# MLP first matrix: seven block products from the third pair of columns on, block differences made in the output projections

## The chip, the cores and the metric

One core of one Trainium2 chip runs the kernel. The metric is device time in microseconds (us), the median of the runs shown. The engines are TensorE (PE: matmuls; PEld is its weight load), VectorE (DVE), ScalarE (ACT), GpSimd (POOL) and the queue of SyncE (SP), which issues the DMAs. Each engine takes its own instructions in order and waits on semaphores. They are listed by a counter's name here: `m_done` counts finished matmul units of an MLP, `m_evac` evacuated plain units, `c_done` sums of block products.

## The reference, cut to what matters

Two layers over 528 positions (16 meta tokens and 512 inputs) of width 1024. Layer 0 mixes with an mLSTM, layer 1 with differential attention; after each comes an MLP with hidden width 4096.

```python
def sq_relu_mlp(y, w_up, w_down):
    u = y @ w_up
    return jnp.square(jax.nn.relu(u)) @ w_down

for i in range(DEPTH):
    y = rmsnorm(h, norm_gains[i, 0])
    y = mixer(y)                      # mLSTM or differential attention, with its output projection
    h = h + y
    h = h + sq_relu_mlp(rmsnorm(h, norm_gains[i, 1]), mlp_w_up[i], mlp_w_down[i])
```

`rmsnorm(h, g)` is `h * rsqrt(mean(h*h) + eps) * g`; the factor of a position is called `rb` below.

## The kernel before, in words

**Number format.** Every fp32 operand is split in a high part (written by ScalarE) and a low part (what VectorE finds left), and a product is three matmuls: high x high, high x low, low x high. `yh, yl` hold the normalised input of the MLP, `ah, al` its squared activations, `hi, lo` the weights of the current pair, `raw` what DMA has loaded. Positions lie along the free dimension, 528 in layer 0 (two spans of 264), the last 512 in layer 1 (one span of 512).

**Pairs.** An MLP is 32 pairs, pair i taking 256 columns of a matrix. They come in four groups of eight: four up pairs (`is_up`, i % 8 < 4), then four down pairs. A *plain* pair is two halves m = 0, 1 of 128 columns, each 8 blocks `kb` x 3 matmuls for each span, in a PSUM bank pair or bank of its own. A *crossed* pair is made as a 2 x 2 block product with seven block products (`PRODUCTS`: A11, A12, S2, S3, S1, S4, A22), each 4 x 3 matmuls over half of the positions (264 or 256). It needs sums and differences of the weight blocks (`form`: S1 to S4, in `lof`), sums and differences of the input's blocks (`th, tl`, made from `tf`), and seven sums of products afterwards (`total`: C11, U2, U3, C22, U4, C12, C21), which put the result into `tb[0]` and `tb[1]`. Product n of a group lies in bank n % 8, so it waits for the sum that read the product eight before it.

**Which are crossed.** `crossed(i)` is an up pair with i >= PLAIN. Before, PLAIN is 8: the four up pairs of group 0 are plain, the twelve of groups 1 to 3 crossed.

**The normalisation.** In group 0 the input is unscaled: `yh, yl` are h times gain, and `evacuate` multiplies by `rb` and takes the ReLU in one operation of VectorE. During group 0 the scaled input is made as well: `scaled_y` (VectorE, `yn`), `y_forms` (VectorE, `tf`), `forms_hi` and `forms_lo` (`th`, `tl`), and at pair 4 `scaled_hi` and `scaled_lo` overwrite `yh, yl` with it. From group 1 on the products need no factor, and ScalarE takes the ReLU of the finished sums in place (`positive`, line 855). Then `squares` on ScalarE writes `abuf` and `ah`, and `act_lo` on VectorE (line 1387) writes `al` and counts `a_ready`.

**The order of the work** is written out by hand: one loop over i on each engine, with the work of neighbouring pairs interleaved. VectorE in iteration i: C21 of pair i-1, `act_lo(i-1, 0)`, `form_lo(i+1, "S23")`, C11 of pair i, `form_lo(i+1, "S14")`, U2, `act_lo(i-1, 1)`, `natural_lo(i+1)`, U3, `natural_lo(i+2)`, C22, U4, forms S1 and S3 of i+2, C12, forms S2 and S4 of i+2. For a plain pair `evacuate` stands at the place of the sums and `plain_lo` at the place of the forms. ScalarE has the high parts in the same order. The first down half of a group (`i % 8 == 4`, m = 0) waits before each block `kb` for `a_ready` of that block (line 1906 is its matmul; 1942 is that of the seven products).

**Before the MLP** stands the output projection (`out_product`): eight units of 48 matmuls (layer 0) or 24 (layer 1) on TensorE; for each VectorE adds the residual to `h`, and `norm_prep` makes `yh, yl` of the block and adds its square to `acc`. After the MLP's first half unit, TensorE sums the squares (`mean_squares`) and ScalarE makes `rb`.

## Time and profile before

| | |
|---|---|
| median of 3 runs | 1241.2 us (1240.85 to 1242.64) |
| the profiled execution | 1241.73 us |
| its span, first to last instruction | 1240.0 us |
| mean granted clock of TensorE | 0.996 of full speed |
| TensorE busy | 1206.2 us |
| VectorE busy | 858.3 us |
| ScalarE busy | 659.7 us |
| read from HBM | 107.38 MB |

All rows come from the one profiled execution. In a timeline the first number is the start in us from the span's start, the second how long it took; consecutive instructions of VectorE overlap a little, so that the spacing of their starts is about 0.08 us shorter than the duration. "Idle before" names who released an instruction that had waited.

### The profile page before, as it was taken

What the parts mean: (1) busy time and instruction counts of PE and PEld (TensorE: products, weight loads), DVE (VectorE), ACT (ScalarE), POOL (GpSimd) and SP (SyncE); (2) the same over time, 40 slices, a digit from 0 to 9 for tenths busy, and PEclk for the clock granted to TensorE, in tenths of its full rate; (3) what the DMA queues carried; (4) which work ended last, traced back from release to release, by engine and by line L of the source; (5) the groups of instructions that cost most, each with busy time, mean ns of one, the idle gap of its engine ahead of it and who ended that gap; (6) DMA issues with size and microseconds to landing.
All of it is one profiled execution on the core that took longest, in us unless ns stands there. A gap on an engine that the chain in (4) does not pass through costs nothing.

```text
span 1240.0 us, 21700 instructions
## 1 busy us (share of the span) xinstructions
PE 1206.2 (97%) x8549; PEld 1127.9 (91%) x8549; DVE 858.3 (69%) x1338; ACT 659.7 (53%) x1111; POOL 66.0 (5%) x105
## 2 busy tenths in 40 slices
PE   6999999999999999999999999998999999999997
PEld 6999999999999999999989998986787998988986
DVE  5778778667668377487468888885776774855852
ACT  4676776543526246246257787775443452543542
POOL 4121120000000000001010000000000000000000
PEclk9999999999999999999999999999999999999999
DMA  6524323232323323323122122212323232342321
GB/s 158 114 74 116 85 69 110 73 96 75 103 80 98 116 83 103 103 75 130 53 85 69 52 68 66 81 40 68 102 102 102 69 128 84 96 129 75 103 69 68
DMA packets 141600, 110.63 MB, mean 89 GB/s; under 512 B 22104, under 2 KB 139920, under 8 KB 141520
## 3 DMA queue, kind: packets, MB, share of 16 engines
q1 hardware_dynamic: 140000, 104.93, 28.1%
q0 software_dynamic: 1392, 4.49, 1.5%
q8 instruction: 56, 0.92, 0.3%
q14 instruction: 24, 0.20, 0.1%
q10 hardware_dynamic: 128, 0.09, 0.0%
HBM read 107.38 MB, written 2.13 MB: 88 GB/s over the span
## 4 chain that ended last, share of the span: by engine, by line
PE 71%; issue 19%; DVE 5%; ACT 3%; POOL 1%; DMA 1%; SPq 0%; DVEq 0%; POOLq 0%; ACTq 0%
PE ps L1906 33%; PE ps L1942 19%; PE ps L1686 15%; PE ps L1736 1%; PE ps L1754 1%; DVE tf L1436 1%; ACT wh L627 1%; DVE wl L1087 1%; DMA raw<-in_mlstm_w_in_dram 1%; DVE tbuf L1397 0%; ACT ah L867 0%; DVE tl L1449 0%; DVE lo L1295 0%; PE ps L1777 0%; PE ps L1789 0%
## 5 line engine op out<-in xcount | busy, mean ns | idle before, releaser
L1906 PE MATMUL ps<-ah,hi 128*128 128x264 f32 (+1 forms) x768 | 205.6, 322 | 3.8 <-DVE al L1387 3.8
L1906 PE MATMUL ps<-al,hi 128*128 128x264 f32 (+1 forms) x768 | 205.3, 322 | 0.0
L1906 PE MATMUL ps<-ah,lo 128*128 128x264 f32 (+1 forms) x768 | 204.8, 321 | 0.0
L627 ACT ACTIVATE hi<-raw 128x1024 fp32r<-128x1024 f32 (+1 forms) x128 | 121.5, 969 | 134.0 <-PE ps L1906 134.0
L1686 PE MATMUL ps<-yh,wh 128*128 128x264 f32 (+1 forms) x704 | 161.1, 303 | 0.0
L1686 PE MATMUL ps<-yl,wh 128*128 128x264 f32 (+1 forms) x704 | 156.0, 296 | 0.0
L1686 PE MATMUL ps<-yh,wl 128*128 128x264 f32 (+1 forms) x704 | 155.7, 295 | 0.0
L1906 PEld LDWEIGHTS ps<-ah,hi 128*128 128x128 f32 x768 | 127.4, 188 | 15.7 <-DVE al L1387 4.5
L1906 PEld LDWEIGHTS ps<-al,hi 128*128 128x128 f32 x768 | 127.5, 188 | 11.1
L1906 PEld LDWEIGHTS ps<-ah,lo 128*128 128x128 f32 x768 | 127.4, 188 | 11.1
L1401 DVE TENSOR_TENSOR h<-ps,h 128x528 f32<-128x528 f32 (+1 forms) x64 | 44.6, 697 | 110.8 <-PE ps L1906 110.8
L1686 PEld LDWEIGHTS ps<-yh,wh 128*128 128x128 f32 x704 | 112.3, 190 | 2.3
L1686 PEld LDWEIGHTS ps<-yh,wl 128*128 128x128 f32 x704 | 111.6, 189 | 2.8
L1686 PEld LDWEIGHTS ps<-yl,wh 128*128 128x128 f32 x704 | 111.8, 189 | 1.6
L1295 DVE TENSOR_TENSOR lo<-raw,hi 128x1024 fp32r<-128x1024 f32 x80 | 97.7, 1223 | 19.2 <-ACT hi L627 18.2
L1942 PE MATMUL ps<-th,hi 128*128 128x264 f32 (+1 forms) x384 | 108.5, 283 | 0.0
L1942 PE MATMUL ps<-tl,hi 128*128 128x264 f32 (+1 forms) x384 | 108.3, 282 | 0.0
L1942 PE MATMUL ps<-th,lo 128*128 128x264 f32 (+1 forms) x384 | 108.2, 282 | 0.0
L1087 DVE TENSOR_TENSOR wl<-raw,wh 128x1024 fp32r<-128x1024 f32 x64 | 79.4, 1241 | 8.1 <-ACT wh L627 6.0
L1942 PE MATMUL ps<-yh,lo 128*128 128x264 f32 (+1 forms) x288 | 81.3, 282 | 0.0
L1942 PE MATMUL ps<-yh,hi 128*128 128x264 f32 (+1 forms) x288 | 81.3, 282 | 0.0
L1942 PE MATMUL ps<-yl,hi 128*128 128x264 f32 (+1 forms) x288 | 81.2, 282 | 0.0
(267 smaller groups left out, 2613.3 us busy)
## 6 DMA issues: line engine op xcount, KB each, us to landing
raw<-in_mlp_w_up_dram SPq DMA_DIRECT2D x32, 1024.0 KB, 5.5
raw<-in_mlp_w_down_dram SPq DMA_DIRECT2D x32, 1024.0 KB, 5.2
raw<-in_diff_w_in_dram SPq DMA_DIRECT2D x24, 512.0 KB, 3.8
raw<-in_mlstm_w_in_dram SPq DMA_DIRECT2D x16, 512.0 KB, 4.6
raw<-in_mlstm_w_in_dram SPq DMA_DIRECT2D x16, 256.0 KB, 5.7
raw<-in_mlstm_w_out_dram SPq DMA_DIRECT2D x3, 1024.0 KB, 5.2
raw<-in_diff_w_out_dram SPq DMA_DIRECT2D x3, 1024.0 KB, 5.2
mbc<-gate_rows POOLq DMA_DIRECT2D x8, 264.0 KB, 5.8
```

The lines of the kernel that those rows point to most:

```text
L627: return nc.scalar.activation(o, i, ACT.Copy, scale=scale)
L1087: V.tensor_tensor(wl[:, k, :, :], raw[:, k // 2, :, P * (k % 2):P * (k % 2) + P], wh[:, k, :, :].bitcast(F32), ALU.subtract).then_inc(spli ...
L1295: V.tensor_tensor(lo[1 - i % 2][:, slots(i, m), :], raw[:, i % 2, :, P * m:P * m + P], hi[1 - i % 2][:, slots(i, m), :].bitcast(F32), ALU. ...
L1401: V.tensor_tensor(tokens(h[:, k, :], spans), src, tokens(h[:, k, :], spans), ALU.add).then_inc(m_evac, 1)
L1436: V.tensor_tensor(tf[:, f, o, 0:w], x, y, ALU.subtract).then_inc(t_made, 1)
L1686: last = mm(ps[:, bank + s, 0:w_], w[:, slot, kb, :], m[:, kb, t0:t0 + w_], start=(kb == 0 and n == 0), stop=(kb == CB - 1 and n == 2))
L1736: last = mm(ps[:, b, c:c + t1 - t0], what(rows, j), p, start=(b not in seen), stop=(n in (1, len(PIECES) - 1) and i == len(passes) - 1))
L1754: last = mm(ps[0:rows, b, c:c + t1 - t0], ks[par][:, s0:s0 + rows], q[:, t0:t1], start=(m == 0), stop=(m == 1))
L1906: last = mm(ps[:, b + s, 0:cw], x[half][:, 20 * m + kb, :], y[:, kb, c0:c0 + cw], start=(kb == 0 and n == 0), stop=(kb == CB - 1 and n == 2))
L1942: last = mm(ps[:, bank, 0:w], x[1 - i % 2][:, row + kb, :], y, start=(kb == 0 and n == 0), stop=(kb == 3 and n == 2))
```

## The change

PLAIN becomes 2: in group 0 only pairs 0 and 1 are plain, pairs 2 and 3 are crossed, 14 crossed pairs for each MLP instead of 12. The input stays unscaled for the whole MLP. Its block differences are made from h and gain by `y_forms` in the output projection, block by block: ScalarE copies `h` times gain into `thf` (two copies for each of the first four blocks), VectorE makes `tf` (one fused operation for each of the first four blocks, three for each of the last four). `forms_hi` and `forms_lo` run beside pairs 0 and 1. `scaled_y`, `scaled_hi` and `scaled_lo` are gone. The factor `rb` is applied to the finished sums: `relu` on VectorE (ReLU and product in one operation) takes the place of `positive` on ScalarE. It stands, for half 1 of pair i-1, behind `form_lo(i+1, "S23")`, and for half 0 of pair i between the forms S2 and S4 of pair i+2. The up halves of pairs 0 and 1 use fewer banks: the fourth half lies where the first was, and a half waits for the evacuation two before it (`c >= 2`). The product S2 of pair 2 waits for all four `tl` and for the evacuation of pair 1's second half.

```diff
--- before.py
+++ after.py
@@ -70,7 +70,7 @@
...
-PLAIN = 8
+PLAIN = 2
 PAIRS = 8 * GROUPS
@@ -105,7 +105,7 @@
...
 FORM = {"S1": 0, "S2": 1, "S3": 2, "A22": 3}
-UP_BANKS = [(0, 2, 4, 6, 0, 2, 4, 6), (4, 5, 7, 6, 4, 5, 7, 6)]
+UP_BANKS = [(0, 2, 4, 0), (4, 5, 4, 5)]
@@ -251,9 +251,10 @@
...
         t_at = w0[0]
+        thf = place("thf", [P, 4, 4, HALF], F32, [arena], limit)
         tl = place("tl", [P, 4, 4, HALF], F32R, w0, limit)
         tf = place("tf", [P, 4, 4, HALF], F32, [t_at], limit)
-        r0, half_at = [ring_at], w0[0]
+        r0 = [ring_at]
         hi, lo, lof = [], [], []
@@ -264,9 +265,6 @@
...
         t1 = place("t1", [P, HALF], F32, w0, limit)
-        yn = [place(f"yn{q}", [P, 2, T], F32, [at + 8 * P * 4], at + 20 * P * 4)
-              for q, at in enumerate((ring_at, ring_at + 28 * P * 4, half_at, half_at + 28 * P * 4))]
         w0 = [a_at]
@@ -337,7 +335,7 @@
...
         m_hi, m_lo, s_made, m_done, c_done, m_relu, m_evac = sems("m_hi m_lo s_made m_done c_done m_relu m_evac")
-        yn_done, t_made, th_done, tl_done, y2_hi, y2_lo, t1_done = sems("yn_done t_made th_done tl_done y2_hi y2_lo t1_done")
+        yt_done, t_made, th_done, tl_done, t1_done = sems("yt_done t_made th_done tl_done t1_done")
@@ -816,6 +814,11 @@
...
                     norm_prep(n, k, spans)
+                    if k < 4:
+                        t0, w = mlp_shape(layer)
+                        for f, n0 in ((2, t0), (3, t0 + w)):
+                            last = copy(thf[:, f, k, 0:w], h[:, k, n0:n0 + w], gains[:, 8 * n + k:8 * n + k + 1])
+                        last.then_inc(yt_done, 1)
@@ -847,12 +850,6 @@
...
                     copy(t1[:, 0:w], ps[:, bank_of(i, "A11"), 0:w]).then_inc(t1_done, 1)
-                def positive(i, m):
-                    b = 8 * (4 * layer + i // 8) + 2 * (i % 8) + m
-                    act.wait_ge(c_done, 7 * ranks + summed(i, "C21" if m else "C12"))
-                    nc.scalar.activation(tb[m][:, t0:T], tb[m][:, t0:T], ACT.Relu).then_inc(m_relu, 1)
@@ -884,16 +881,10 @@
...
-                def scaled_hi(q):
-                    act.wait_ge(yn_done, 8 * layer + 8)
-                    act.wait_ge(m_done, items + DONE[3, 1])
-                    copy(yh[:, 2 * q:2 * q + 2, t0:T], yn[q][:, :, t0:T]).then_inc(y2_hi, 1)
                 def forms_hi(n):
-                    act.wait_ge(t_made, 8 * layer + 2 * n + 2)
-                    f = (0, 2, 1, 3)[n]
+                    act.wait_ge(t_made, 16 * layer + 16)
+                    f = (2, 1, 0, 3)[n]
                     copy(th[:, f, :, 0:w], tf[:, f, :, 0:w]).then_inc(th_done, 1)
@@ -905,8 +896,6 @@
...
                         snap(i)
-                    if crossed(i - 1):
-                        positive(i - 1, 1)
                     if crossed(i + 1):
@@ -920,12 +909,9 @@
...
                         finish(i, 0)
-                    if i == 3:
-                        for n in range(4):
-                            forms_hi(n)
-                    if i == 4:
-                        for q in range(4):
-                            scaled_hi(q)
+                    if i < 2:
+                        forms_hi(2 * i)
+                        forms_hi(2 * i + 1)
                     if i + 2 < PAIRS:
@@ -934,7 +920,6 @@
...
                     if crossed(i):
-                        positive(i, 0)
                         squares(i, 0)
@@ -1304,13 +1289,28 @@
...
                     norm_prep(n, k, spans)
+                    y_forms(layer, n, k)
+            def y_forms(layer, norm, k):
+                t0, w = mlp_shape(layer)
+                kb, gain, made = k % 4, gains[:, 8 * norm + k:8 * norm + k + 1], 16 * layer
+                first, second = h[:, k, t0:t0 + w], h[:, k, t0 + w:T]
+                if k < 4:
+                    dve.wait_ge(yt_done, 4 * layer + k + 1)
+                    V.scalar_tensor_tensor(tf[:, 0, kb, 0:w], second, gain, thf[:, 2, kb, 0:w],
+                                           ALU.mult, ALU.subtract).then_inc(t_made, 1)
+                else:
+                    dve.wait_ge(t_made, made + kb + 1)
+                    for f, x, other in ((1, second, tf[:, 0, kb, 0:w]), (2, second, thf[:, 3, kb, 0:w]), (3, first, tf[:, 1, kb, 0:w])):
+                        if f == 3:
+                            dve.wait_ge(t_made, made + 4 + 3 * kb + 1)
+                        V.scalar_tensor_tensor(tf[:, f, kb, 0:w], x, gain, other, ALU.mult, ALU.subtract).then_inc(t_made, 1)
...
                 items, ranks, norm = layer * N_DONE, layer * N_CROSSED, 2 * layer + 1
-                gain = lambda kb: gains[:, 8 * norm + kb:8 * norm + kb + 1]
                 def form(i, name, after):
@@ -1320,8 +1320,6 @@
...
                     if name == "S1":
-                        if i in (8, 9):
-                            dve.wait_ge(y2_lo, 4 * layer + 4)
                         dve.wait_ge(m_raw[i % 2], 16 * (PAIRS // 2 * layer + i // 2 + 1))
@@ -1380,6 +1378,11 @@
...
+                def relu(i, m):
+                    dve.wait_ge(c_done, 7 * (ranks + RANK[i] - 1) + SUMS["C21" if m else "C12"])
+                    V.scalar_tensor_tensor(tb[m][:, t0:T], tb[m][:, t0:T], 0.0, rb[:, t0:T], ALU.max, ALU.mult).then_inc(m_relu, 1)
                 def act_lo(i, m):
@@ -1413,39 +1416,11 @@
...
-                def scaled_y(b0):
-                    dve.wait_ge(unit_done, (U_OUT0, U_OUT1)[layer] + 8)
-                    dve.wait_ge(evac, (U_OUT0, U_OUT1)[layer] + 8)
-                    dve.wait_ge(rb_ready, norm + 1)
-                    for b in range(b0, b0 + 4):
-                        V.scalar_tensor_tensor(yn[b // 2][:, b % 2, t0:T], h[:, b, t0:T], gain(b), rb[:, t0:T],
-                                               ALU.mult, ALU.mult).then_inc(yn_done, 1)
-                def y_forms(n):
-                    f = (0, 2, 1, 3)[n]
-                    if n < 2:
-                        dve.wait_ge(yn_done, 8 * layer + 8)
-                    else:
-                        dve.wait_ge(t_made, 8 * layer + (2, 6)[n - 2])
-                    for q in range(2):
-                        top, low, o = yn[q], yn[2 + q], slice(2 * q, 2 * q + 2)
-                        x, y = ((top[:, :, mid:T], top[:, :, t0:mid]), (low[:, :, mid:T], top[:, :, mid:T]),
-                                (low[:, :, mid:T], tf[:, 0, o, 0:w]), (low[:, :, t0:mid], tf[:, 1, o, 0:w]))[n]
-                        V.tensor_tensor(tf[:, f, o, 0:w], x, y, ALU.subtract).then_inc(t_made, 1)
-                def scaled_lo(q):
-                    dve.wait_ge(y2_hi, 4 * layer + q + 1)
-                    V.tensor_tensor(yl[:, 2 * q:2 * q + 2, t0:T], yn[q][:, :, t0:T],
-                                    yh[:, 2 * q:2 * q + 2, t0:T].bitcast(F32), ALU.subtract).then_inc(y2_lo, 1)
                 def forms_lo(n):
-                    f = (0, 2, 1, 3)[n]
+                    f = (2, 1, 0, 3)[n]
                     dve.wait_ge(th_done, 4 * layer + n + 1)
-                    dve.wait_ge(t_made, 8 * layer + 8)
+                    dve.wait_ge(t_made, 16 * layer + 16)
                     V.tensor_tensor(tl[:, f, :, 0:w], tf[:, f, :, 0:w], th[:, f, :, 0:w].bitcast(F32), ALU.subtract).then_inc(tl_done, 1)
@@ -1460,6 +1435,8 @@
...
                         form_lo(i + 1, "S23")
+                    if crossed(i - 1):
+                        relu(i - 1, 1)
                     if crossed(i):
@@ -1479,18 +1456,9 @@
...
                         if is_up(i):
-                            if i < 2:
-                                scaled_y(4 * i)
                             act_lo(i, 0)
-                            if i == 2:
-                                for n in range(4):
-                                    y_forms(n)
-                            if i == 3:
-                                for n in range(4):
-                                    forms_lo(n)
-                        elif i == 4:
-                            for q in range(4):
-                                scaled_lo(q)
+                            forms_lo(2 * i)
+                            forms_lo(2 * i + 1)
                     after = crossed(i + 2)
@@ -1508,6 +1476,9 @@
...
                         form(i + 2, "S2", 1)
+                    if crossed(i):
+                        relu(i, 0)
+                    if after:
                         form(i + 2, "S4", 3)
@@ -1885,10 +1856,8 @@
...
                         pe.wait_ge(evac, u_out + 5 + 2 * i + m)
-                    if c >= 4:
+                    if c >= 2:
                         pe.wait_ge(m_evac, plains + c - 1)
-                    if (i, m) == (1, 1):
-                        pe.wait_ge(ln_done, norm + 1)
                     if crossed(i - 1) and m == 0:
@@ -1914,22 +1883,24 @@
...
                         pe.wait_ge(m_lo, ready + READY[i, group])
-                    if i == 8 and name == "A11":
-                        pe.wait_ge(y2_lo, 4 * layer + 4)
-                    if i == 8 and name == "S2":
+                    if i == PLAIN and name == "A11":
+                        pe.wait_ge(ln_done, norm + 1)
+                        pe.wait_ge(evac, u_out + 8)
+                    if i == PLAIN and name == "S2":
+                        pe.wait_ge(m_evac, plains + 4)
                         pe.wait_ge(tl_done, 4 * layer + 4)
-                    if n >= 8:
+                    if n >= 8 and i - i % 8 + (n - 8) // 7 >= PLAIN:
...
                             pe.wait_ge(c_done, 7 * ranks + summed(last, FREED[product_]))
-                    elif n >= 4:
+                    elif 4 <= n < 8:
...
                         pe.wait_ge(m_evac, plains + PLAINS[u // 2, u % 2])
-                    elif n == 0 and i > 8:
+                    elif n == 0:
                         pe.wait_ge(c_done, 7 * (ranks + RANK[i] - 1))
...
                     for kb in range(4):
```

## Rows read from the trace of the kernel before

**Rows 1.** The page, part 1: busy time and share of the span, each engine.

```profile
PE 1206.2 (97%) x8549; PEld 1127.9 (91%) x8549; DVE 858.3 (69%) x1338; ACT 659.7 (53%) x1111; POOL 66.0 (5%) x105
```

**Rows 2.** The chain that ended last: start us, us, what; both MLPs.

```profile
274.17 23.37 PE ps L1906 x192
...
451.26 40.77 PE ps L1942 x336
492.03 46.76 PE ps L1906 x384
...
888.11 22.32 PE ps L1906 x96
...
974.26 39.69 PE ps L1942 x336
1013.96 44.63 PE ps L1906 x192
```

**Rows 3.** Waits of TensorE: us in total, times, longest.

```profile
PE ps L1906 <- DVE al L1387: 3.8, 2, 2.2
```

**Rows 4.** Timeline of VectorE: start us, us, instruction, idle time before it.

```profile
460.50 0.42 DVE L1381 TENSOR_TENSOR tbuf<-u,ps 128x264 f32<-128x264 f32 x1
460.84 0.68 DVE L1328 TENSOR_TENSOR lof<-lof,raw 128x512 f32<-128x512 f32 x1
...
462.17 0.42 DVE L1381 TENSOR_TENSOR tbuf<-u,ps 128x264 f32<-128x264 f32 x1
462.85 0.71 DVE L1387 TENSOR_TENSOR al<-abuf,ah 128x528 fp32r<-128x528 f32 x1 [0.25 <-ACT ah L867]
463.87 1.23 DVE L1335 TENSOR_TENSOR lo<-lof,hi 128x1024 fp32r<-128x1024 f32 x1 [0.31 <-ACT hi L627]
465.01 0.42 DVE L1381 TENSOR_TENSOR tbuf<-t,ps 128x264 f32<-128x264 f32 x1
...
467.11 0.70 DVE L1387 TENSOR_TENSOR al<-abuf,ah 128x528 fp32r<-128x528 f32 x1
467.73 0.68 DVE L1342 TENSOR_TENSOR lo<-raw,hi 128x512 fp32r<-128x512 f32 x1
468.33 0.42 DVE L1381 TENSOR_TENSOR u<-u,ps 128x264 f32<-128x264 f32 x1
...
474.03 0.71 DVE L1387 TENSOR_TENSOR al<-abuf,ah 128x528 fp32r<-128x528 f32 x1 [0.26 <-ACT ah L867]
...
494.79 0.71 DVE L1387 TENSOR_TENSOR al<-abuf,ah 128x528 fp32r<-128x528 f32 x1 [1.04 <-ACT ah L867]
...
1017.12 0.69 DVE L1387 TENSOR_TENSOR al<-abuf,ah 128x512 fp32r<-128x512 f32 x1 [1.01 <-ACT ah L867]
```

**Rows 5.** Timeline of VectorE, output projection and first pairs of the MLPs.

```profile
239.68 0.43 DVE L1098 COPY acc<-abuf 128x528 f32<-128x528 f32 x1
...
275.69 0.71 DVE L1397 SCALAR_TENSOR_TENSOR tbuf<-ps,rb 128x528 f32<-128x528 f32 x1 [1.00 <-ACT rb L663]
...
282.73 0.71 DVE L1387 TENSOR_TENSOR al<-abuf,ah 128x528 fp32r<-128x528 f32 x1 [1.25 <-ACT ah L867]
...
313.30 4.76 DVE L1449 TENSOR_TENSOR tl<-tf,th 128x1056 fp32r<-128x1056 f32 x4 [0.27 <-ACT th L627]
...
889.60 0.69 DVE L1397 SCALAR_TENSOR_TENSOR tbuf<-ps,rb 128x512 f32<-128x512 f32 x1 [2.53 <-issue]
```

**Rows 6.** Groups of instructions by form: busy us, mean ns of one.

```profile
L1258 DVE SCALAR_TENSOR_TENSOR acc<-acc,of 128x528 f32<-128x528 f32 x8 | 5.6, 701 | 0.7 <-ACT acc L779 0.7
...
L855 ACT ACTIVATE tbuf<-tbuf 128x528 f32<-128x528 f32 x24 | 15.4, 640 | 46.8 <-DVE tbuf L1381 46.8
```

**Rows 7.** Windows near the start: busy of each engine, granted clock, DMA.

```profile
core 0: us, PE busy (x) PEld busy (x) DVE busy (x) ACT busy (x) POOL busy (x), PEclk, DMA share, GB/s
...
42.00:46.00 4.00, 2.17 (x19) 1.63 (x18) 3.20 (x6) 3.74 (x9) 2.06 (x4) 1.00 0.30 69
46.00:50.00 4.00, 4.00 (x24) 3.92 (x23) 2.76 (x4) 3.87 (x10) 0.21 (x1) 0.57 1.02 236
```

## The prediction

> **What bounds the kernel now.** I read the page first: TensorE is busy 97% of the 1240.0 us span [rows 1], so only what shortens its stream, or makes it wait, moves the end. Next the chain that ended last, merged in time [rows 2]: in both MLPs it is almost nothing but TensorE. Four crossed pairs (7 block products of 12 matmuls each, 336 in all) take 40.77 us in layer 0 and 39.69 us in layer 1; eight plain halves take 46.76 and 44.63 us. Then the waits [rows 3]: in 64 pairs TensorE stood still twice, 3.8 us together, both for `al`, the low parts of the activations (once in group 0 of each layer). Last VectorE's timeline, since the change gives VectorE work. VectorE is only 69% busy over the span [rows 1], but inside four crossed pairs it goes from one operation to the next with hardly a gap: from one `al` to the corresponding one of the next pair it needs 462.85 to 474.03, 11.18 us [rows 4], while TensorE needs 40.77/4 = 10.19 us for the pair. It gains its lateness back only in the plain pairs that follow. This is the place to look at.
>
> **1. Matmuls removed.** Pairs 2 and 3 of both layers become crossed. A plain pair costs 46.76/4 = 11.69 us (layer 0) and 44.63/4 = 11.16 (layer 1), a crossed one 10.19 and 9.92 [rows 2]. Gain 1.50 x 2 + 1.24 x 2 = 5.5 us, all on TensorE's path.
>
> **2. The old wait.** The two waits of TensorE for `al` in group 0 [rows 3] came from a VectorE queue that carried `scaled_y`, the old `y_forms`, `forms_lo` and `scaled_lo` between pairs 0 and 4. Those are gone or moved ahead. Behind pair 3 VectorE's queue now holds two crossed pairs only, and if TensorE has waited in pair 2 (below), VectorE is level with it there. Gain 3.8 us.
>
> **3. Block differences in the output projections.** ScalarE gets 8 copies of 264 elements, VectorE 16 fused operations of about 0.38 us each (a 264-element sum is spaced 0.34 us, from 460.50 to 460.84 [rows 4]; a pointer scalar adds a little). VectorE gets at most three more per output block, 1.1 us, under 5.8 us of matmuls for a block, so TensorE covers it. Only the last three matter: they push VectorE's two splits of pair 1 behind them, so that the first evacuation begins at about 275.8 instead of 275.69 [rows 5]. Uncovered it would be 1.1 us per layer; the 0.1 is in part 4's sum, and layer 1 has room until its factor is ready.
>
> **4. VectorE's opening queue.** Pair 2's third product, S2, needs the evacuation of pair 1's second half, its bank; before, that half had a bank of its own and nothing waited. On VectorE it now stands behind all the preparation of pairs 2 and 3. Spacings, from one start to the next: evacuation to `al` 0.70 + 1.25 (wait for ScalarE's two squares) = 1.95 [rows 5]; `al` to the first `tl` 0.71 + 0.27 = 0.98; two `tl` 2 x 4.76/4 = 2.38; a 1024-element low part 1.14; forms S1 and S3 2 x 0.60; S2 and S4 1.33 (460.84 to 462.17) [rows 4]. A block is 8.98 us. Between the two blocks lie evacuation 0.62, two 1024-element low parts 2.28, `al` 0.62, a 512-element one 0.60: 4.12. So the evacuation of pair 1's second half starts at 275.8 + 8.98 + 4.12 + 8.98 = 297.9 and S2 may start at 298.65. TensorE is there at 274.17 + 3 x 5.85 + 2 x 1.46 = 294.6 [rows 2]. **Wait: 4.0 us.** In layer 1: 889.60 [rows 5] + 22.1 less some 0.3 for the shorter rows + 0.75 = 912.1, against 888.11 + 3 x 5.58 + 2 x 1.42 = 907.7: **4.4 us**. Together 8.4. Bounds for each: 2.5 us less if VectorE need not wait for ScalarE's squares (1.25 us, twice), 0.6 more if its steps are 2.5% longer.
>
> **5. The ReLU moves from ScalarE to VectorE.** ScalarE loses 0.64 us, VectorE gets a two-source fused operation over 528 elements; the same form, L1258, takes 0.701 us [rows 6], spacing about 0.62. What is queued behind it: `relu(i,0)` stands between the forms S2 and S4 of pair i+2, and the squares on ScalarE and then `al` wait for it. From its start to `al` is 0.70 + 1.25 = 1.95 us. From `al` of one pair to the next `relu(i,0)` there are, by the spacings of [rows 4]: 1.02 + 1.14 + 0.62 (`relu(i-1,1)`) + 0.34 + 1.14 + 0.34 + 0.62 + 0.60 + 0.34 + 1.14 + 0.68 + 1.20 + 0.34 + 0.60 = 10.12 us. So a full iteration takes 12.07 us, not 11.18, against TensorE's 10.19. Following the group that starts at 451.26: the first ReLU at 461.44, its `al` at 463.4; the second pair's at 475.5; the third (no forms to make: 7.98 to C12, 0.47 for C12 to end, 1.95) at 485.9; then ReLU and `al` of its second half, the last at 488.4; splits and sums 1.02 + 3.30 to C12 of the fourth pair at 492.75; ReLU 493.2, `al` 495.2, ReLU 495.8, last `al` 497.7, done 498.45. Before, that last `al` began at 494.79 [rows 4]: 2.95 us earlier. The first down half needs it for its eighth block, at 492.03 + 7/8 x 5.85 = 497.1 [rows 2]. The old margin of 1.6 us becomes a **wait of 1.4 us**, in each of three groups. Layer 1: last `al` at 1017.12 + 2.95, done 0.75 later at 1020.8, needed at 1013.96 + 4.88 = 1018.8: 2.0 us, and a few tenths more, as its crossed pairs are 0.27 us shorter and VectorE's steps hardly are: **2.3 us**. Together 3 x 1.4 + 3 x 2.3 = 11.1 us. From both sides: with the one-source COPY of the same 528 elements as the nearest other row, 0.43 us [rows 5], eight ReLUs would be 2.2 us shorter in the chain and about 0.8 us of the 2.95 remained, inside the margin: 0. With every step 2.5% longer it is about 5 us more than my sum. I take the fused row, the same form and size. ScalarE's idle time does not help; it waits for VectorE already.
>
> The row says that ReLU costs 0.640 us on ScalarE and 0.701 on VectorE [rows 6]. The Trainium skill, "ScalarE: Activation LUTs", Rules for kernel authors, says to use VectorE, not ScalarE, for ReLU and multiplication. By that rule the move would cost nothing and part 5 would be 0; here the form is two-source fp32 and the busier engine gets it, so I go by the row.
>
> **6. The clock.** The windows show the granted clock at 1.00 through 42 to 46 us, where TensorE was busy for 2.17 of 4 us, and 0.57 in the 4 us after, a mixture of 2.4 and 1.2 GHz [rows 7]: 0.43 x 4 = 1.7 us lost. A wait of 4 us in part 4 may cause the same, twice; in the MLP before, waits of up to 2.2 us [rows 3] did not show it. Bounds 0 and 3.4; I take one fall, 1.7 us. The Trainium skill, "TensorE: Matmul & The Clock Gate", Part 1, says that an idle array falls back to half rate; by that it would be both, 1.7 us more.
>
> **The sum.** -5.5 - 3.8 + 8.4 + 11.1 + 1.7 = +11.9 us. The span would be 1251.9, the profiled execution, 1241.73, 1253.6, and the median, which is 0.5 us lower (1241.2), **1253**. SP's loads for pairs 2 to 5 start when the last split of the buffer is done and have 5 to 7 us before use, as later groups have now; I give them nothing.
>
> **Rivals.** (a) **Forecast**, both VectorE delays reach TensorE: 0.74. (b) **Faster**: VectorE's backlog is drained before TensorE meets it, so only parts 1 and 2 count, 1241.2 - 9.3 = 1232. Place: VectorE's queue between the first evacuation and S2, and in the last of four crossed pairs. It decides when 4.0 of the 22.1 us of part 4 vanish and 1.5 of the 2.95 of part 5. For it: ScalarE is relieved, and part of VectorE's spacing is waiting for it. Against it: ScalarE's squares still follow the ReLU, and the steps are measured ones. 0.06. (c) **Only one of the two**: no wait in part 5, as with the one-source price: about 1242; or none in part 4: -9.3 + 11.1, 1243. 0.10, nearly all of it within 0.2% of 1241.2. (d) **The lateness grows**: VectorE's steps 2.5% longer put `al` late for the seventh block too, and delay the second half of pair 1: 1259 or more. [...] 0.10. That the seven products do not save their matmuls I leave out: they do so in 12 pairs per layer now [rows 2].
>
> **Range and chances.** 0.2% of the time, 2.5 us, is about what this kernel's measurement can tell. (a) alone covers 1249 to 1257: below, no fall of the clock and half of part 4's 5 us; above, two falls, 1.2 more in part 4 and 0.2 for each of the six groups. With half of (d) the range is 1247 to 1259. Faster by over 0.2%: 0.06, (b). Within: 0.08, from (c). Slower: 0.86.
>
> **What would show it.** Right: the waits view has S2 of pair 2 (th products) waiting some 4 us for VectorE, twice; six waits for `al` of 1 to 2.5 us, at the start of the down pairs of groups 1 to 3; none in group 0; crossed pairs still 10.2 and 9.9 us; ReLU on VectorE at 0.70 us; the clock below 1.00 after one of the 4 us waits. Wrong: no wait of TensorE at `al`, or VectorE reaching C21 with idle time in front of it in the second pair of a group; or waits inside the crossed pairs for banks, which I give none, since the sums stay within eight products.

## The result, and the profile after

The median of 6 runs is 1261.32 us (1259.09 to 1266.43); the kernel before, run 6 times beside it, has 1241.92 (1240.85 to 1242.79). The ratio is 1.0152, with a 95% interval of 1.0135 to 1.0169: **slower by 19.4 us**. The forecast was 1253, range 1247 to 1259. The direction was right and the time lies 2.3 us above the range.

The profiled execution took 1260.07 us, with a span of 1258.4. Page, part 1, of the kernel after:

```profile
PE 1207.8 (96%) x8597; PEld 1130.7 (90%) x8597; DVE 896.5 (71%) x1430; ACT 638.9 (51%) x1083; POOL 63.7 (5%) x105
```

Against [rows 1], VectorE has 38 us more and ScalarE 21 us less. TensorE runs 48 matmuls more (12 fewer for each new crossed pair of layer 0, 36 more, but half as wide, for each of layer 1) and is busy 1.6 us longer, though its columns are fewer: some of them run at a lower clock. Now its waits. The waits view, TensorE:

```profile
PE ps L1875 <- DVE al L1390: 11.0, 10, 1.6
PE ps L1913 <- DVE tbuf L1400: 4.2, 1, 4.2
PE ps L1913 <- issue: 4.0, 1, 4.0
...
PE ps L1875 <- DVE tbuf L1400: 0.6, 1, 0.6
```

Line 1875 is the plain matmul, 1913 that of the seven products, 1390 is `act_lo`, 1400 `evacuate`. Where [rows 3] had two waits and 3.8 us, there are 19.8 us now. Timeline of TensorE, the rows with a wait inside the MLPs (those of group 2 of layer 1, at 1114.68 and 1117.19, repeat the two of group 1):

```profile
297.95 0.56 PE L1913 MATMUL ps<-th,hi 128*128 128x264 f32 x1 [3.98 <-issue]
412.17 0.51 PE L1875 MATMUL ps<-ah,hi 128*128 128x264 f32 x2 [1.57 <-DVE al L1390]
501.62 0.51 PE L1875 MATMUL ps<-ah,hi 128*128 128x264 f32 x2 [1.58 <-DVE al L1390]
589.15 0.52 PE L1875 MATMUL ps<-ah,hi 128*128 128x264 f32 x2 [0.46 <-DVE al L1390]
591.73 0.51 PE L1875 MATMUL ps<-ah,hi 128*128 128x264 f32 x2 [1.57 <-DVE al L1390]
...
907.32 0.47 PE L1875 MATMUL ps<-yh,hi 128*128 128x512 f32 x1 [0.59 <-DVE tbuf L1400]
920.15 0.36 PE L1913 MATMUL ps<-th,hi 128*128 128x256 f32 x1 [4.17 <-DVE tbuf L1400]
1027.85 0.50 PE L1875 MATMUL ps<-ah,hi 128*128 128x512 f32 x1 [0.43 <-DVE al L1390]
1030.36 0.50 PE L1875 MATMUL ps<-ah,hi 128*128 128x512 f32 x1 [1.55 <-DVE al L1390]
...
1201.50 0.50 PE L1875 MATMUL ps<-ah,hi 128*128 128x512 f32 x1 [0.33 <-DVE al L1390]
1204.02 0.76 PE L1875 MATMUL ps<-ah,hi 128*128 128x512 f32 x1 [1.55 <-DVE al L1390]
```

The two rows at `th` are S2 of pair 2. In layer 0 the view names "issue" as what ended the wait; the evacuation that S2 waits for ended just then, as the timeline of VectorE shows (it started at 297.15). The row at 907.32 is the last of the four plain up halves of layer 1, which waits for its bank. The others are the first down half behind four crossed pairs. Its block 8, which needs the last `al`, waits 1.6 us in groups 1 to 3 of both layers, and in four of these six its block 7 has waited 0.3 to 0.5 us, 2.5 to 2.6 us earlier. Timeline of VectorE, the evacuation of pair 1's second half in each layer, and in the group that starts at 453.93 the ReLUs and low parts:

```profile
297.15 0.70 DVE L1400 SCALAR_TENSOR_TENSOR tbuf<-ps,rb 128x528 f32<-128x528 f32 x1
...
464.27 0.70 DVE L1384 SCALAR_TENSOR_TENSOR tbuf<-tbuf,rb 128x528 f32<-128x528 f32 x1
...
466.22 0.71 DVE L1390 TENSOR_TENSOR al<-abuf,ah 128x528 fp32r<-128x528 f32 x1 [0.30 <-ACT ah L864]
...
476.34 0.70 DVE L1384 SCALAR_TENSOR_TENSOR tbuf<-tbuf,rb 128x528 f32<-128x528 f32 x1
...
500.86 0.71 DVE L1390 TENSOR_TENSOR al<-abuf,ah 128x528 fp32r<-128x528 f32 x1 [1.24 <-ACT ah L864]
...
919.37 0.68 DVE L1400 SCALAR_TENSOR_TENSOR tbuf<-ps,rb 128x512 f32<-128x512 f32 x1
```

Read the two ReLUs of half 0: 476.34 - 464.27 = 12.07 us, which is VectorE's time for a crossed pair; TensorE's is 10.19. Read the last `al` from the group's first matmul: 500.86 - 453.93 = 46.93 us. Before, it was 494.79 [rows 4], and the group's first matmul is at 451.10 in the timeline (451.26 in the chain of [rows 2], which enters it a little later): 43.69, 3.24 us less. And the clock, windows of the kernel after around S2 in layer 0 (columns as in [rows 7]):

```profile
292.00:296.00 4.00, 1.97 (x17) 1.75 (x15) 4.00 (x6) 1.03 (x2) 0.00 (x0) 1.00 0.13 46
296.00:300.00 4.00, 2.05 (x9) 2.08 (x10) 3.96 (x6) 3.46 (x6) 0.00 (x0) 0.52 0.02 6
300.00:304.00 4.00, 4.00 (x24) 4.00 (x23) 2.70 (x6) 1.36 (x2) 0.00 (x0) 0.63 0.04 6
304.00:308.00 4.00, 4.00 (x35) 4.00 (x34) 3.03 (x6) 0.50 (x1) 0.00 (x0) 1.00 0.76 257
```

TensorE stands still from about 294 to 297.95, and the granted clock is 0.52 and 0.63 in the eight microseconds from 296 on: mostly the lower level, 1.2 GHz, then 2.4 GHz again. The same happens behind the 4.17 us wait of layer 1 and once more in its last group, from 1204 to 1210 (0.91 and 0.75 in two windows of 5 us). Inside the MLPs of the kernel before the clock never fell. Near the start it is the other way round: there the kernel before has the fall of [rows 7], and the windows 46 to 50 and 50 to 54 us of the kernel after are at 1.00.

**Where the 18.4 us of span went**, from the first matmuls of the stages in both traces. Fewer matmuls: -5.5. The two old waits: -4.4. The waits of S2: 4.2 and 4.3. The four plain up halves of layer 1, with the new wait of 0.59 us at 907.32: 1.0. The down pairs behind crossed ones: 1.9, 1.9 and 2.5 in layer 0, three times 2.5 in layer 1, 13.8 together. Three falls of the clock: 2.2 + 1.6 + 1.5 = 5.3. The MLP of layer 0 starts 0.65 earlier. The sum is 18.1. Whether the fall near the start has a part in the 0.65 is open: of the profiled executions here, those with one such fall (the kernel before and experiments 2, 3, 4, 6) start this MLP at 266.2 to 267.3, those with none (the kernel after and experiment 8) at 266.7.

### The profile page after: what moved, and what is told of

The parts are those of the page before. It is cut to its first block and busy times, and to the rows that moved or that the text cites. A ratio compares the mean times of both kernels' runs of the same rounds, so it can differ in the third digit from the quotient of the medians.

```text
span 1258.4 us, 21898 instructions
## 1 busy us (share of the span) xinstructions
PE 1207.8 (96%) x8597; PEld 1130.7 (90%) x8597; DVE 896.5 (71%) x1430; ACT 638.9 (51%) x1083; POOL 63.7 (5%) x105
## 5 line engine op out<-in xcount | busy, mean ns | idle before, releaser
L1913 PE MATMUL ps<-th,hi 128*128 128x264 f32 (+1 forms) x448 | 128.6, 287 | 8.2 <-DVE tbuf L1400 4.2
L1913 PE MATMUL ps<-tl,hi 128*128 128x264 f32 (+1 forms) x448 | 128.1, 286 | 0.0
L1913 PE MATMUL ps<-th,lo 128*128 128x264 f32 (+1 forms) x448 | 128.0, 286 | 0.0
L863 ACT ACTIVATE abuf<-tbuf 128x528 f32<-128x528 f32 (+1 forms) x64 | 40.9, 638 | 170.8 <-DVE tbuf L1384 164.8
L1280 DVE TENSOR_TENSOR lo<-raw,hi 128x1024 fp32r<-128x1024 f32 x72 | 87.9, 1224 | 18.8 <-ACT hi L625 17.6
L1913 PE MATMUL ps<-yh,lo 128*128 128x264 f32 (+1 forms) x336 | 94.9, 282 | 0.0
L1913 PE MATMUL ps<-yh,hi 128*128 128x264 f32 (+1 forms) x336 | 94.8, 282 | 0.0
L1913 PE MATMUL ps<-yl,hi 128*128 128x264 f32 (+1 forms) x336 | 94.7, 282 | 0.0
```

The costliest lines, as they stand in the source:

```text
L863: nc.scalar.activation(ab[m][:, t0:T], tb[m][:, t0:T], ACT.Square).then_inc(sqa_done, 1)
L1280: V.tensor_tensor(lo[1 - i % 2][:, slots(i, m), :], raw[:, i % 2, :, P * m:P * m + P], hi[1 - i % 2][:, slots(i, m), :].bitcast(F32), ALU. ...
L1913: last = mm(ps[:, bank, 0:w], x[1 - i % 2][:, row + kb, :], y, start=(kb == 0 and n == 0), stop=(kb == 3 and n == 2))
```

## The experiments

Two theories. **A**: VectorE's queue sets the end in two places, in front of S2, where bank and evacuation meet, and in front of `al`, where the ReLU stands in the way; all else follows from the order of the queue. **B**: VectorE simply has too much to do in a crossed pair, in any order, or the new products of pairs 2 and 3 are dearer than counted. The kernel before had a median of 1242.74 us beside experiments 1 to 4 and of 1242.80 us beside 5 to 8.

**1. ReLU back on ScalarE**, without the factor `rb` of these sums.

```diff
@@ ScalarE @@
+                    if crossed(i - 1):
+                        positive(i - 1, 1)
...
                     if crossed(i):
+                        positive(i, 0)
                         squares(i, 0)
@@ VectorE @@
-                    if crossed(i - 1):
-                        relu(i - 1, 1)
...
-                    if crossed(i):
-                        relu(i, 0)
```

> The changed kernel with the ReLU of the crossed pairs back on ScalarE, at its old places; the factor rb of these activations is left out. Theory A (both VectorE delays are real and separate, and the clock falls after waits): TensorE's waits for al in front of the down pairs, 11.0 us in ten, go to 0; the waits for S2 of pair 2 (8.2 us) and for the evacuation in pair 1 (0.6 us) stay, with a fall of the clock of 1.7 us behind each of the two long ones. About 1241.9 - 5.5 - 3.8 + 8.8 + 3.4 = 1245 us. Rival B (the seven products of pairs 2 and 3 save less than 5.5 us, or the work moved to the output projections costs TensorE time): the waits go as in A, but the time stays above 1250. Rival C (the waits for al come from the opening, not from the ReLU): they stay, above 1257.

Measured: 1244.83 us (1243.29 to 1247.37), ratio 1.0014 [1.0005, 1.0024]. No wait for `al` is left, S2 still waits 4.0 and 4.2 us, and the clock still falls behind both. The last `al` of a group starts at 43.70 us from the group's first matmul. So the ReLU's move to these places costs 1261.3 - 1244.8 = 16.5 us, and the rest of the change costs about 2. B's second half, dearer products, is gone: where no wait and no fall comes, pairs 2 and 3 of layer 0 take 20.37 us together (first matmuls of the stages, experiment 4), twice the 10.19 of a crossed pair.

**2. Other banks for the first pairs of layer 0, and S2 in both layers without the wait for the evacuation of pair 1's second half.**

```diff
-UP_BANKS = [(0, 2, 4, 0), (4, 5, 4, 5)]
+UP_BANKS = [(0, 2, 0, 4), (4, 5, 4, 5)]
...
-                    if c >= 2:
+                    if c >= 2 and (layer, c) != (0, 3):
                         pe.wait_ge(m_evac, plains + c - 1)
...
                     if i == PLAIN and name == "S2":
-                        pe.wait_ge(m_evac, plains + 4)
+                        pe.wait_ge(m_evac, plains + 3)
                         pe.wait_ge(tl_done, 4 * layer + 4)
+                    if i == PLAIN and name == "A22":
+                        pe.wait_ge(m_evac, plains + 4)
```

> The changed kernel with another bank for the second half of pair 1, so that S2 of pair 2 waits only for the evacuation before, and A22 of pair 2 for the last one. Theory A (VectorE's queue is behind by 4 us at this point whatever TensorE waits for): the 4 us waits at S2 go, but TensorE then meets the same lateness at the first down half of group 0, as waits for al of its seventh and eighth block, together 3.1 us in layer 0 and 3.6 in layer 1; only 1.8 us are saved, and the clock falls less often: 1256 to 1260 us. Rival B (the S2 wait is a matter of one bank): the waits go and nothing comes in their place, 1261.3 - 8.2 - 3.4 = 1249.7 us.

Measured: 1257.21 us (1255.72 to 1260.54), ratio 1.0125 [1.0109, 1.014]. The waits of S2 are gone, with 8.2 us in them, and the time fell by only 4. In layer 1 no bank was changed, and none had to be: by `UP_BANKS` that half lies in bank 5 there, and S2 of pair 2 in bank 0 (product 16, modulo 8). Its wait of 4.17 us was for a condition of the code that S2 does not need. The waits view of this kernel and its new rows in the timeline of TensorE show why:

```profile
PE ps L1875 <- DVE al L1390: 16.7, 14, 1.6
```

```profile
316.62 0.51 PE L1875 MATMUL ps<-ah,hi 128*128 128x264 f32 x2 [1.07 <-DVE al L1390]
319.19 0.81 PE L1875 MATMUL ps<-ah,hi 128*128 128x264 f32 x2 [1.57 <-DVE al L1390]
...
936.67 0.51 PE L1875 MATMUL ps<-ah,hi 128*128 128x512 f32 x1 [1.48 <-DVE al L1390]
939.18 0.51 PE L1875 MATMUL ps<-ah,hi 128*128 128x512 f32 x1 [1.54 <-DVE al L1390]
```

Group 0 had no wait for `al` after the change; it has four now, 5.7 us more in total. The wait of S2 had let VectorE catch up. Taken away, its lateness goes on to the next place where TensorE meets it: the down pairs of group 0 take 51.27 us where the kernel after has 46.76, and 49.78 in layer 1 where it has 44.63. The clock falls there too (0.88 and 0.78 in the windows from 315 to 325, 0.66 from 940 to 945).

**3. The ReLU of half 1 directly behind C21**, one step earlier in the same queue, the same work.

```diff
                         total(i - 1, "C21")
+                        relu(i - 1, 1)
...
                         form_lo(i + 1, "S23")
-                    if crossed(i - 1):
-                        relu(i - 1, 1)
```

> The changed kernel with relu(i-1, 1) one place up in VectorE's order: directly behind the sum C21 of pair i-1, ahead of act_lo(i-1, 0) and form_lo(i+1, S23). The same instructions, the same durations. Theory A (the place in the queue decides: the squares of the second half run while VectorE works on the first): the waits for al, 11.0 us, go to below 1 us, the waits for S2 stay: 1244 to 1247 us. Rival B (VectorE's total of work decides, 28 ReLUs of 0.70 us for each layer): nothing changes, 1259 us or more.

Measured: 1244.41 us (1243.58 to 1247.09), ratio 1.0014 [1.0005, 1.0024]. This one line takes 16.9 us away. The fused ReLU still runs on VectorE, 707 ns each. Timeline of VectorE of this kernel, the end of a group whose first matmul is at 451.18 (C21 of a pair, its ReLU, the two `al`):

```profile
492.15 0.43 DVE L1379 TENSOR_TENSOR tbuf<-u,ps 128x264 f32<-128x264 f32 x1 [0.20 <-PE ps L1912]
492.61 0.71 DVE L1384 SCALAR_TENSOR_TENSOR tbuf<-tbuf,rb 128x528 f32<-128x528 f32 x1
493.24 0.70 DVE L1390 TENSOR_TENSOR al<-abuf,ah 128x528 fp32r<-128x528 f32 x1
494.56 0.71 DVE L1390 TENSOR_TENSOR al<-abuf,ah 128x528 fp32r<-128x528 f32 x1 [0.63 <-ACT ah L864]
```

The ReLU of half 1 now comes before `al` of half 0, so ScalarE squares half 1 while VectorE makes that `al`. In the kernel after it came behind it, and VectorE then stood 1.24 us for ScalarE. The last `al` starts 43.38 us from the group's start instead of 46.93. A full iteration is shorter as well: the ReLUs of half 0 stand at 461.53 and 472.97, 11.44 us apart instead of 12.07. B's first half has fallen: the work is the same, the place decides. At this place the move from ScalarE costs nothing that can be told (experiment 1 has 1244.83 us), though VectorE's 11.44 are still more than TensorE's 10.19: over four pairs the lateness stays inside the margin.

**4. Experiments 2 and 3 together, the other ReLU early as well**, directly behind C12, and one low part of the second down pair behind the last `al` (beside the lines of experiments 2 and 3):

```diff
                         total(i, "C12")
+                        relu(i, 0)
                     if after:
                         form(i + 2, "S2", 1)
-                    if crossed(i):
-                        relu(i, 0)
...
                     elif 1 <= i < PAIRS - 1:
+                        if crossed(i - 1) and not crossed(i):
+                            plain_lo(layer, i + 1, 0)
                         plain_lo(layer, i + 1, 1)
...
-                    elif i + 2 < PAIRS:
+                    elif i + 2 < PAIRS and not (crossed(i) and not crossed(i + 1)):
                         plain_lo(layer, i + 2, 0)
```

> The changed kernel with four reorderings and no work added or left out: the banks of e2, the ReLU places of e3, relu(i, 0) directly behind C12, and the low part of the second pair of down columns moved behind the last al. Theory A: no wait of TensorE above 0.5 us in either MLP, no fall of the clock there: 1241.9 - 5.5 - 3.8 + 0.6 = 1233 us. Rival B (the waits come back somewhere else in VectorE's order, or the clock falls anyhow): 1237 us or more, and the waits view names the place.

Measured: 1233.43 us (1231.94 to 1233.56), ratio 0.9923 [0.9909, 0.9936]. No wait for `al` and none of S2 is left, and no clock below 1.00 inside the MLPs. This beats both kernels.

**5. The kernel before, with its ReLUs on VectorE at the places of the change.** The product with `rb` comes along, on data already scaled.

```diff
@@ ScalarE @@
-                    if crossed(i - 1):
-                        positive(i - 1, 1)
...
-                        positive(i, 0)
@@ VectorE @@
                         form_lo(i + 1, "S23")
+                    if crossed(i - 1):
+                        relu(i - 1, 1)
...
                         form(i + 2, "S2", 1)
+                    if crossed(i):
+                        relu(i, 0)
```

> The kernel before, with one part of the change alone: the ReLU of the crossed pairs on VectorE with the factor rb, at the two places of the change (the activations are already scaled there, so the factor comes in once too often). Pairs 2 and 3 stay plain. Theory A (this move alone makes the late al of groups 1 to 3): the two old waits for al in group 0 stay (3.8 us), ten new ones of 11 us come in groups 1 to 3, which cost 12 to 13 us with the restart of the stream; the clock falls after one to three of them, 1.7 us each: 1242.3 + 12.3 + 3 = about 1257 us (1254 to 1260). Rival B (the al waits need the longer run of crossed pairs or the unscaled input of the change): below 1248 us.

Measured: 1261.24 us (1259.88 to 1262.44), ratio 1.015 [1.0135, 1.0166], more than expected: this part alone costs 18.4 us. Its waits view has

```profile
PE ps L1913 <- DVE al L1389: 14.8, 12, 2.2
```

that is 11.0 us more than [rows 3] (line 1913 is the plain matmul here). The rest is the lost overlap (below) and the clock. Two pairs of waits of this run, and windows around each, timeline and windows:

```profile
1027.20 0.50 PE L1913 MATMUL ps<-ah,hi 128*128 128x512 f32 x1 [0.42 <-DVE al L1389]
1029.70 0.50 PE L1913 MATMUL ps<-ah,hi 128*128 128x512 f32 x1 [1.54 <-DVE al L1389]
...
1114.02 0.50 PE L1913 MATMUL ps<-ah,hi 128*128 128x512 f32 x1 [0.42 <-DVE al L1389]
1116.53 0.64 PE L1913 MATMUL ps<-ah,hi 128*128 128x512 f32 x1 [1.54 <-DVE al L1389]
```

```profile
1026.00:1032.00 6.00, 4.04 (x17) 2.67 (x16) 3.95 (x6) 3.57 (x5) 0.00 (x0) 1.00 0.02 7
...
1116.00:1120.00 4.00, 3.47 (x9) 2.69 (x10) 3.18 (x4) 1.76 (x2) 0.00 (x0) 0.59 0.18 54
```

The same two waits, 0.42 and 1.54 us, leave the clock at 1.00 in one group and bring it down in the next. From first down matmul to the next group these pairs took 47.13 and 48.71 us: a fall costs 1.6. There are three inside this run's MLPs (942, 1117 and 1205).

The one at 942 comes behind an old wait, the single one of group 0 in layer 1. The kernel before has the same wait with no fall behind it. Timeline and windows, first of the kernel before, then of this run:

```profile
931.65 0.39 PE L1906 MATMUL ps<-ah,lo 128*128 128x512 f32 x1
934.23 0.50 PE L1906 MATMUL ps<-ah,hi 128*128 128x512 f32 x1 [2.18 <-DVE al L1387]
```

```profile
934.00:938.00 4.00, 3.77 (x16) 3.10 (x17) 3.75 (x5) 4.00 (x5) 0.00 (x0) 1.00 0.28 75
```

```profile
941.33 0.50 PE L1913 MATMUL ps<-ah,hi 128*128 128x512 f32 x1 [2.19 <-DVE al L1389]
```

```profile
941.00:945.00 4.00, 3.67 (x11) 2.99 (x12) 3.75 (x5) 4.00 (x5) 0.00 (x0) 0.71 0.28 87
```

So one stop of 2.2 us left the clock at 1.00 in one execution and brought it down in the other. The down pairs of this group took 47.11 us in the kernel before and 48.64 in this run, 1.5 more. What decides between the two is not shown.

**6. The ReLU in a cheaper form at the changed places**: one source, no factor.

```diff
-                    V.scalar_tensor_tensor(tb[m][:, t0:T], tb[m][:, t0:T], 0.0, rb[:, t0:T], ALU.max, ALU.mult).then_inc(m_relu, 1)
+                    V.tensor_scalar(tb[m][:, t0:T], tb[m][:, t0:T], 0.0, None, ALU.max).then_inc(m_relu, 1)
```

> The changed kernel with the ReLU of the crossed pairs as a one-source operation on VectorE (maximum with 0; the factor rb is left out), at the same places. Theory A (an al is late by the sum of what stands ahead of it, and each ReLU counts with its length): if it takes about 0.43 us as the copy of the same size does, the waits for al in layer 0 go and those in layer 1 shrink to 0.3 us per group; the waits at S2 stay: 1244 to 1247 us. Rival B (the detour over VectorE's queue costs, not the length): the waits for al stay above 8 us together, 1256 us or more.

Measured: 1246.69 us (1245.4 to 1247.21), ratio 1.0034 [1.0022, 1.0046]. Groups by form, first of the kernel after, then of this one:

```profile
L1384 DVE SCALAR_TENSOR_TENSOR tbuf<-tbuf,rb 128x528 f32<-128x528 f32 x28 | 20.0, 713 | 0.3
L1384 DVE SCALAR_TENSOR_TENSOR tbuf<-tbuf,rb 128x512 f32<-128x512 f32 x28 | 19.2, 686 | 0.3
```

```profile
L1384 DVE TENSOR_SCALAR tbuf<-tbuf 128x528 f32<-128x528 f32 x28 | 12.4, 444 | 0.3
L1384 DVE TENSOR_SCALAR tbuf<-tbuf 128x512 f32<-128x512 f32 x28 | 11.8, 421 | 0.3
```

0.27 us less for each ReLU brings the last `al` of the group at 451.32 from 46.93 to 44.74 and leaves a single wait of 0.30 us in layer 0; in layer 1 the down pairs are 0.41 us longer than in [rows 2]. It shows the edge: 14.6 us hang on eight times 0.27 us in a group.

**7. Experiment 3 with TensorE kept busy in front of S2**: 32 matmuls whose results nobody reads, in each layer.

```diff
                     if i == PLAIN and name == "S2":
+                        pe.wait_ge(m_evac, plains + 3)
+                        for _ in range(32):
+                            mm(ps[:, 4, 0:w], hi[1 - i % 2][:, 4 * SLOT["S2"], :], yh[:, 0, t0:t0 + w], start=True, stop=True)
                         pe.wait_ge(m_evac, plains + 4)
```

> The kernel of e3 (only the two long waits at S2 of pair 2 are left) with 32 matmuls more in each MLP, 264 or 256 columns, whose result nobody reads, issued in the time in which TensorE waits there. Theory A (behind each long wait the granted clock falls, at 1.7 us each): the waits view shows well under 1 us at this place, the granted clock stays 1.00 in both windows, and with 64 matmuls more the kernel is 2 to 4 us faster than e3's 1244.4: 1241 to 1242.5 us. Rival B (the clock costs nothing that can be seen; S2 starts when VectorE allows it): the same as e3, 1244.4, or slower by what the matmuls overrun.

Measured: 1241.86 us (1240.73 to 1243.36), ratio 0.9991 [0.9982, 1.0]: with 64 matmuls more it is 2.5 us faster than experiment 3. The chain of experiment 3, from S2 of pair 2 to the end of pair 3, and that of this kernel:

```profile
297.84 19.21 PE ps L1912 x144
...
912.91 18.65 PE ps L1912 x144
```

```profile
295.29 3.89 PE ps L1891 x32
299.22 17.71 PE ps L1915 x144
...
912.70 17.23 PE ps L1915 x144
```

The same 144 matmuls take 1.50 and 1.42 us less when the time ahead of them is filled (line 1891 is the filling), and the granted clock stays at 1.00 through 286 to 308 and 906 to 926 us. Those 2.9 us are the price of the two falls, with the slower start behind each stop in them (the first two matmuls of S2 start 0.36 us apart in the kernel after, the next 0.22).

**8. Experiments 2 and 3 together, and nothing else.**

> The changed kernel with two of e4's four edits: the bank of pair 1's second half, and relu(i-1, 1) directly behind C21. Theory A: in groups 1 to 3 no wait for al is left, in group 0 two or three of 0.3 to 0.5 us; 1241.9 - 5.5 - 3.8 + 0.6 + 1.2 = 1234.4 us. Rival B (the other two edits carried the gain of e4): 1237 us or more.

Measured: 1233.91 us (1233.02 to 1235.09), ratio 0.9932 [0.9916, 0.9947]. One wait for `al` of 0.27 us is left, and the 0.58 of the plain halves in layer 1. The interval overlaps that of experiment 4, so the times do not tell what the two steps added there are worth. The traces do in part: in experiment 4 the down pairs of group 0 are 0.45 us shorter in layer 0 (46.76 against 47.21) and 0.93 in layer 1 (44.63 against 45.56). These two edits, five lines of waits and banks and one line of order, are enough to beat the kernel before by 8.9 us.

## Why the prediction was wrong

It had the places, and for VectorE's queue the mechanism; two terms of its sum were too small, and the larger miss is the clock.

- **Part 1**, -5.5: right. Crossed pairs take 40.77 and 39.69 us after the change as before it.
- **Part 2**, -3.8: right. No wait for `al` is left in group 0; in stage times it was worth 4.4. But experiment 2 shows that this depends on S2's wait, which lets VectorE catch up, as the text supposed.
- **Part 3**, 0: right as far as it can be seen; the first evacuation started at 275.18, and the MLP of layer 0 no later.
- **Part 4**, +8.4: right. The forecast had the evacuation start at 297.9 and waits of 4.0 and 4.4; they are 297.15, and 3.98 and 4.17. In TensorE's stage times they cost 8.5. The reason given, that S2 needs the bank of pair 1's second half, holds for layer 0 only; in layer 1 it is the code's wait that holds S2 back, not a bank (experiment 2). Not foreseen was the 0.59 us wait of the plain halves of layer 1 for their banks, worth 1.0.
- **Part 5**, +11.1: right in kind, too small in layer 0. The chain of VectorE was worked out well: a full iteration of 12.07 us came out at 12.07, the last `al` 3.24 us later instead of 2.95. Layer 0 has idle rows of 1.57 us against the 1.4, but its down pairs grew by 1.9, 1.9 and 2.5 us, and those of layer 1 by 2.5 instead of 2.3: 13.8 us in all. Two things were mis-sized. `al` was late for block 7 too in four of the six groups, where the text had one wait for each. And a wait costs more than its idle row: matmuls that follow each other overlap, and each stop loses that overlap (0.3 us for one stop of 1.57, 0.5 for two of 0.43 and 1.55). The rows of the kernel before in experiment 5 show it: a matmul of 0.39 us, in a stream whose starts are 0.23 us apart, starts at 931.65; the next would have started at 931.88 and came at 934.23, 2.35 us late with an idle row of 2.18. Experiments 1, 3 and 5 hold this part up from three sides: 16.5, 16.9 and 18.4 us, each with its falls of the clock.
- **Part 6**, +1.7: **this is the step that failed.** It took one fall out of a possible two, since waits of up to 2.2 us had not shown one before. Both waits of S2 brought the clock down, in every kernel that kept them and left them empty, and then there was a third fall in a place to which the text gave none, behind the short waits for `al`. Together 5.3 us in the profiled run instead of 1.7. Its premise, that waits of up to 2.2 us do not bring the clock down, rested on one execution: in experiment 5 it fell behind the same wait of 2.19 us. The Trainium skill's rule that an idle array falls back to half rate ("TensorE: Matmul & The Clock Gate", Part 1), which the text quoted and set aside, was the better guide for both waits of S2; the trace agrees with it there.

So 3.6 us come from part 6, 2.7 from part 5 and 1.0 from the plain halves; 0.6 more than forecast was gained by the old waits and 0.65 at the start. That makes 6.1 of the 6.5 us between the span's 18.4 and the forecast 11.9. The median stands another 1.2 us above the profiled execution where the forecast had it 0.5 below, and the number of falls seems to differ from run to run: the six runs have mean granted clocks of 0.986 to 0.992, and the slowest, 1266.43 us, has the lowest. That its additional 6.4 us are four more falls behind the `al` waits is argued from 1.6 us for each, not shown in a trace. The range ended at 1259 because it had two falls at most, and 0.2 us more for each of the six groups in part 5, where 2.7 came in all.

Of the rivals, (b) did not come: no lateness vanished. (d) has the measured time, 1259 or more, and one of its signs, `al` late for the seventh block too (four of six groups), but not its cause: the iteration is the forecast 12.07 us, with no step longer. (c) with the one-source price was put at about 1242; experiment 6 made that case and came out at 1246.7: a second fall (1.5 us or so), 1.2 us in the down pairs of layer 1 and 1.0 in its plain halves come on top, 3.7 of the 4.7. The rule that ReLU belongs on VectorE ("ScalarE: Activation LUTs", Rules for kernel authors, in the Trainium skill), for which the page gives bf16 with one source as the reason, does not hold for the form used here: 0.713 us there against 0.640 on ScalarE [rows 6]. With one source it does, 0.444 us (experiment 6). At the places of the change the move cost 16.5 us all the same, and one line further up nothing.

## What to carry to other kernels

When work moves to another engine, walk that engine's queue through the whole period and compare it with the bound engine's period, even if its busy share is only 70%; then ask for the earliest place in the queue at which the moved step can stand, since one line further up was worth 16.9 of 1261 us. For each wait on an evacuation, ask which bank it guards: one of the two at S2 guarded none. A wait that is removed passes its lateness to the next meeting place, so edits at both places have to be measured together (4 us for the one, 16.9 for the other, 27.4 for both). Count a stop of TensorE with what follows it: the lost overlap and the clock.

## What the runs showed of the hardware

- Each idle stretch of TensorE of 4.0 to 4.2 us in an MLP was followed by the lower clock for the next few microseconds, 1.4 to 2.2 us lost, in the kernel after and in experiments 1, 3 and 6. Filled with matmuls (experiment 7) it was not.
- Pairs of stops of 0.3 to 0.5 and 1.5 to 1.6 us, 2.5 to 2.6 us apart, sometimes did the same (1.6 us) and sometimes not, with the same two waits in one execution (experiment 5). So did a single stop of 2.2 us: no fall in the kernel before, one in experiment 5 (1.5 us).
- Times scatter with no such pair of stops as well: from lowest to highest 7.3 us in 6 runs of the kernel after, 4.6 us in 21 runs of the kernel before. One source is seen near the start: in the profiled executions of experiments 1, 5 and 7 the clock is low from 45 to 52 us (0.50 in 46 to 50, 0.76 to 0.79 in 50 to 54 in experiments 1 and 7), twice as long as in the others that have this fall, and the first MLP starts at 268.0 to 268.4 us instead of 266.2 to 267.3.
- A ReLU of 528 fp32 elements on VectorE takes 0.444 us with one source and 0.713 with two; on ScalarE it takes 0.640 us.
